# Block 1: the dilated attention's output projection in split products instead of f32 products

## The reference, cut to what matters

```python
ret = retention(rq, rk, rv, rg)
att = dilated_attention(aq, ak, av, rel_bias)
merged = jax.nn.sigmoid(ga) * (ret @ w_ret_o[l]) + jax.nn.sigmoid(gb) * (att @ w_att_o[l])
x = x + gt_a[:, None, :] * (merged @ w_o[l])
```

## Time and profile before

| | |
|---|---|
| median of 3 runs | 3548.91 us (3545.66 to 3554.22) |
| profiled execution, its own time | 3551.16 us |
| its span | 3549.2 us |
| mean granted PE clock over the span | 0.977 of full speed |
| PE busy | 3373.7 us, 95% of the span |
| DVE, ACT, POOL busy | 2045.4, 1772.0, 1048.0 us |

### The profile page before, as it was taken

The page is one execution under the profiler, slowest core; times in us unless marked ns, Lnnn a source line. Parts: engine busy times, 40 slices in busy tenths (PEclk is TensorE's granted clock), DMA queues, the critical chain, the costliest instruction groups (busy, mean ns, idle before and its releaser), DMA issues. The chain is left out here.

```text
span 3549.2 us, 54751 instructions
## 1 busy us (share of the span) xinstructions
PE 3373.7 (95%) x20660; PEld 2727.9 (77%) x20660; DVE 2045.4 (58%) x2356; ACT 1772.0 (50%) x2340; POOL 1048.0 (30%) x432
## 2 busy tenths in 40 slices
PE   7999999989999999999999898999999987799997
PEld 5888777768888888888888683778887866678876
DVE  3320121279999999999999725511153155446665
ACT  3222333258887878887888634432233342233333
POOL 2334222313222232323232140144443300034443
PEclk9999999989999999999999999999999988999999
DMA  8223443359999999999999637123322310022221
GB/s 288 85 72 101 125 125 125 112 207 383 375 381 374 385 368 386 367 386 371 381 378 377 249 111 280 66 83 97 99 89 72 101 37 4 7 72 95 96 95 42
DMA packets 247186, 696.26 MB, mean 196 GB/s; under 512 B 19806, under 2 KB 151634, under 8 KB 188420
## 3 DMA queue, kind: packets, MB, share of 16 engines
q1 hardware_dynamic: 237140, 658.52, 49.9%
q0 software_dynamic: 9792, 35.66, 3.8%
q10 hardware_dynamic: 112, 0.03, 0.0%
HBM read 668.90 MB, written 29.71 MB: 197 GB/s over the span
## 5 line engine op out<-in xcount | busy, mean ns | idle before, releaser
L340 POOL TENSOR_TENSOR split_w<-ring,split_w 128x1024 fp32r<-128x1024 f32 (+1 forms) x294 | 702.1, 2389 | 1581.6 <-ACT split_w L335 1505.3
L2272 DVE TENSOR_TENSOR moe_low<-ring,moe_high 128x2048 fp32r<-128x2048 f32 x408 | 929.4, 2285 | 56.6 <-ACT moe_high L2262 51.5
L2262 ACT ACTIVATE moe_high<-ring 128x1024 fp32r<-128x1024 f32 x810 | 833.6, 1063 | 123.4 <-PE psum L2513 121.9
L335 ACT ACTIVATE split_w<-ring 128x1024 fp32r<-128x1024 f32 (+1 forms) x294 | 304.4, 1036 | 978.4 <-PE psum L540 596.7
L2509 PE MATMUL psum<-moe_high,moe_xe 128*128 128x512 f32 x2176 | 585.2, 391 | 0.0
L2509 PEld LDWEIGHTS psum<-moe_high,moe_xe 128*128 128x128 f32 x2176 | 409.5, 188 | 82.2
L2421 POOL DMA_INDIRECT moe_y_rows<-moe_ye,moe_target x33 | 193.5, 5863 | 658.4 <-DVE moe_ye L2328 658.4
L540 PE MATMUL psum<-pair,split_w 128*128 128x512 f32 x1488 | 337.9, 389 | 0.0
L2513 PE MATMUL psum<-moe_low,moe_xe 128*128 128x512 f32 x1088 | 336.5, 390 | 0.1
L540 PEld LDWEIGHTS psum<-pair,split_w 128*128 128x128 f32 x1488 | 279.2, 188 | 58.8 <-issue 0.9
L540 PE MATMUL psum<-b_pair,split_w 128*128 128x512 f32 x1344 | 309.4, 391 | 0.0
(11 more groups left out here) (643 smaller groups left out, 4286.0 us busy)
## 6 DMA issues: line engine op xcount, KB each, us to landing
ring<-in_w_experts SPq DMA_DIRECT2D x408, 1024.0 KB, 8.7
ring<-in_w_mod SPq DMA_DIRECT2D x48, 1024.0 KB, 6.1
ring<-in_w_in SPq DMA_DIRECT2D x39, 1024.0 KB, 5.3
ring<-in_w_up SPq DMA_DIRECT2D x33, 1024.0 KB, 5.1
ring<-in_w_in SPq DMA_DIRECT2D x44, 512.0 KB, 5.2
ring<-in_w_down SPq DMA_DIRECT2D x20, 1024.0 KB, 5.1
ring<-in_w_gate SPq DMA_DIRECT2D x11, 1024.0 KB, 5.3
ring<-in_w_out SPq DMA_DIRECT2D x8, 1024.0 KB, 5.2
```

The costliest lines, as they stand in the source:

```text
L335: self.nc.scalar.activation(high, raw, ACT.Copy).then_inc(self.K.rounded, 1)
L340: self.nc.gpsimd.tensor_tensor(low, raw, high.bitcast(F32), ALU.subtract).then_inc(self.K.split, 1)
L2262: self.nc.scalar.activation(self.B["high"][:, j % HALVES, :], self.raw(j), ACT.Copy).then_inc(self.high, 1)
L2272: self.nc.vector.tensor_tensor(flat(self.low_of(j, 2)), self.K.ring[:, self.ring_slot(j // 2), :], high, ALU.subtract).then_inc(self.low, 2)
```

## The change

`att_o` joins `SPLIT`. Its weights (two chunks, four halves) are split as those of the other stages are; the first half is then split at the end of `gate_b`, and in `attention_out` ACT and POOL have the other three halves to split before they come to those of `w_o`. The rows of `attT` are split in `gate_b`: a new class `AttentionSplit` puts one Copy on ACT and one subtraction on DVE (128x512 each) into the steps (1, 0), (1, 1), (2, 0) and (2, 1). They go to a new tensor `b1_att_pair` (16 KB in each partition, beside `gb`). The projection's 32 f32 matmuls become 96 split ones, 24 to a half. PE waits for the last low part of `attT`, and for each half of the weights.

```diff
-SPLIT = ("ret", "gate_a", "ret_o", "att", "gate_b", "w_o", ...
+SPLIT = ("ret", "gate_a", "ret_o", "att", "gate_b", "att_o", "w_o", ...
...
+class AttentionSplit:
+    def __init__(self, K, attT, high, whole):
+        self.K, self.nc, self.attT, self.whole = K, K.nc, attT, whole
+        self.parts = (high[:, 0, :, :], high[:, 1, :, :])
+        self.high_at, self.low_at = {}, {}
+
+    def act_step(self, sc, j, i):
+        if j in (1, 2):
+            k = 2 * (j - 1) + i
+            if k == 0:
+                self.whole(sc)
+            self.K.act_link(self.nc.scalar.activation(self.parts[0][:, k, :], self.attT[:, k, :], ACT.Copy))
+            self.high_at[k] = self.K.act_order_n
+
+    def dve_step(self, ve, j, i):
+        if j in (1, 2):
+            k = 2 * (j - 1) + i
+            ve.wait_ge(self.K.act_order, self.high_at[k])
+            self.K.dve_link(self.nc.vector.tensor_tensor(self.parts[1][:, k, :], self.attT[:, k, :],
+                                                         self.parts[0][:, k, :].bitcast(F32), ALU.subtract))
+            self.low_at[k] = self.K.dve_order_n
...
-    linear_split(K, stage, "T", pair, 1, vacated=vacated,
+    linear_split(K, stage, "T", pair, 1, vacated=vacated, loads=loads, asked=True,
...
-def attention_out(K, attT, merge, source, vacated):
+def attention_out(K, x, merge, source, vacated):
...
-    ahead, evac0 = SplitAhead(K, last), K.dve_evac_n
+    W, evac0 = SplitWeights(K, "att_o"), K.dve_evac_n
...
         def _(sc):
-            ahead.high_ahead(sc)
+            for n, pieces in W.halves.items():
+                for _, _, place in pieces:
+                    W.act_high(sc, n, place)
+            W.high_ahead(sc)
             source.weights_high(sc)
             sc.wait_ge(K.dve_evac, evac0 + 1)
             for i in range(source.done):
...
         def _(po):
-            ahead.low_ahead(po)
+            W.pool(po)
             source.weights_low(po)
...
         def _(pe):
+            pe.wait_ge(K.dve_order, x.low_at[AH - 1])
             for j in range(2):
-                K.wait_chunk(pe, first + j)
                 vacated(pe, j)
-                w = K.slot(first + j)
-                for i in range(4):
-                    for k in range(AH):
-                        ins = nc.tensor.matmul(K.ps[:, 4 * j + i, :], w[:, k, i * P:(i + 1) * P], attT[:, k, :],
-                                               start=(k == 0), stop=(k == AH - 1))
-                ins.then_inc(K.chunk_used, 1)
+                for r0, nr, place in W.halves[first + j]:
+                    w = W.ready(pe, first + j, place)
+                    for i in range(4):
+                        for k in range(nr):
+                            for a, b in ((0, 0), (1, 0), (0, 1)):
+                                ins = nc.tensor.matmul(K.ps[:, 4 * j + i, :], w[:, a, k, i * P:(i + 1) * P],
+                                                       x.parts[b][:, r0 + k, :], start=(r0 + k + a + b == 0),
+                                                       stop=(r0 + k == AH - 1 and b == 1))
+                    W.used(ins, place)
             pe.wait_ge(K.dve_evac, evac0 + 1)
             source.products(pe)
```

More of the change, by code:

```diff
@@ L41 @@
 RWKV_C = 32
-SPLIT = ("ret", "gate_a", "ret_o", "att", "gate_b", "w_o", "b2_qkv", "b2_rest", "b2_out", "b2_up", "b2_down",
+SPLIT = ("ret", "gate_a", "ret_o", "att", "gate_b", "att_o", "w_o", "b2_qkv", "b2_rest", "b2_out", "b2_up", "b2_down",
          "b3_qk", "b3_v", "b3_rw", "b3_out", "b3_up", "b3_down")
@@ L1628, in retention, with sigmoid_gate @@
     return bias, vacated
-def sigmoid_gate(K, stage, pair, dst, vacated=None, room=None):
+def sigmoid_gate(K, stage, pair, dst, vacated=None, room=None, loads=None):
     def act(j, banks):
@@ L1954, in emptied @@
             pe.wait_ge(copied, 4 * AH)
-    return emptied
+    return emptied, lambda eng: eng.wait_ge(copied, 4 * AH)
+class AttentionSplit:
[17 more added lines that the diff above has]
+            self.low_at[k] = self.K.dve_order_n
 class RouteTables:
@@ L2813, in block1 @@
                                        lambda i: at_head + ATT_CHUNKS * (i // 2) + 5 + 2 * (i % 2), (7, 2), (0, 6))
-                        emptied = dilated(K, pair, attT, T0, T12, M, tables,
+                        emptied, whole_attT = dilated(K, pair, attT, T0, T12, M, tables,
                                           lambda pe, j: pe.wait_ge(K.dve_evac, dve0 + j + 1))
-                    with nc.sbuf_tensor("b1_gate_b", [P, KD, S], F32) as gb:
+                    with nc.sbuf_tensor("b1_gate_b", [P, KD, S], F32) as gb, \
+                            nc.sbuf_tensor("b1_att_pair", [P, 2, AH, S], F32R) as att_pair:
+                        parts = AttentionSplit(K, attT[:, :, :], att_pair[:, :, :, :], whole_attT)
                         act1, dve1 = K.act_evac_n, K.dve_evac_n
-                        sigmoid_gate(K, "gate_b", pair, gb, emptied, M.mods_ready)
+                        sigmoid_gate(K, "gate_b", pair, gb, emptied, M.mods_ready, parts)
                         def merge(j, banks):
@@ L2826, in block1 @@
                         source = SourceAhead(K, "w_o", merged, pair, 2)
-                        attention_out(K, attT, merge, source, lambda pe, j: pe.wait_ge(K.act_evac, act1 + 2 * j + 2))
+                        attention_out(K, parts, merge, source, lambda pe, j: pe.wait_ge(K.act_evac, act1 + 2 * j + 2))
             K.mods3 = K.later_ctx.enter_context(nc.sbuf_tensor("b3_mods", [P, 4, KD], F32, side="right"))
```

## The result

| | before | after |
|---|---|---|
| median | 3547.51 us (3542.89 to 3554.22, 19 runs) | 3554.69 us (3551.03 to 3558.66, 19 runs) |
| profiled execution, span | 3551.16, 3549.2 us | 3557.4, 3555.6 us |
| mean granted PE clock in the profiled execution | 0.977 | 0.975 |

The ratio is 1.0023, 95% interval [1.0017, 1.0029]: the changed kernel is **slower by 7 to 8 us** (the medians lie 7.18 apart; 0.0023 x 3548 is 8.2). The median lies 0.3 us inside the predicted range, which is luck: the range was made wide for other rivals and for scatter, not for this cause.

The account below looks back on a forecast made before the run. The prediction took PE's own work to bound the kernel. Matmuls −5.72, stall +5.0 and clock +1.72 summed to +1.0 us, a median of 3549.9 us, range 3545.0 to 3555.0.

Parts of the forecast that it names:

- The matmuls: Attention output projection on PE: four groups of 24 split matmuls take 21.76 us instead of 27.48, 5.72 us earlier.
- The rows of attT in the gate: Four ACT Copies and four DVE subtractions fit into idle time in the gate; cost 0, otherwise 2.5 us.
- The weights: Splitting the projection's weight halves on ACT and POOL: each is ready before PE asks; cost 0.
- Where PE then waits: Ahead of L457, PE idles 5.0 us for `w_o`'s place 1 and `merged`'s piece 0, with POOL holding DVE.
- The clock: In L457 behind the idle gap, PE falls to half rate and loses 1.72 us; bounds 0 and twice that.
- The sum: Whole program: −5.72 + 5.0 + 1.72 = +1.0 us, median 3549.9 us.
- 1: Ahead of L457, the stall comes without the clock's fall: −0.7 us, 3548.2; chance 0.15.
- 2: At the projection's end, PE doesn't wait and the whole gain arrives: −5.7 us, 3543.2; chance 0.06.
- 3: In the projection, the first merge holds POOL, making half 3 late: +2.8 us, 3551.7; chance 0.05.
- 4: In the dense output projection, the clock stays down: +9.1 us, 3558.0; chance 0.04.

Follow-up runs that it names:

- r3: Changed kernel with ACT splitting `merged` ahead of the weights that wait for the projection's last matmul; 0.9998 of the kernel before.
- r4: Changed kernel with 20 unread matmuls of 128x512 filling PE's gap ahead of L457; 1.0016 of the kernel before.
- s3: Changed kernel with 96 small unread matmuls in PE's gap ahead of L457, 128 more than the kernel before; 1.0003 of the kernel before.
- r2: Changed kernel run again unchanged, for a second trace; 1.0023 of the kernel before.
- s1: Kernel before the change with 32 small unread 32x32 matmuls ahead of L457; 1.0021 of the kernel before.
- t1: Changed kernel with ACT splitting `merged` first, plus 96 small matmuls where PE waits in block 1's routing; 0.9980 of the kernel before, median 3541.31 us.
- s4: Changed kernel with ACT splitting `merged` first, plus 96 small unread matmuls ahead of L457; 0.9998 of the kernel before.
- s2: Kernel before the change with 128 small unread matmuls ahead of L457; 1.0013 of the kernel before.

## Why the prediction was wrong, point by point

- **The matmuls**: right. −5.72 predicted; without the stall the stretch gives −5.75 (r3).
- **The rows of attT in the gate**: right, cost 0. DVE's subtractions took 0.69 to 2.48 us and were through near 640, as said.
- **The weights**: right. PE waited for no half inside the projection.
- **Where PE then waits**: right, instruction by instruction, an idle 4.81 us for 5.0; that POOL holds DVE was the better of the two bounds.
- **The clock**: right in kind, 1.48 for 1.72. r4 shows that the gap brought it on: with large matmuls in it L457 takes 5.72. With small ones in it the clock fell all the same (s3: 7.30).
- **The sum**: this is the step that failed. Its +1.0 us is the stretch's, and the stretch took +0.71 and +1.44. The step carried it over to the program as if nothing outside could change; the 32 matmuls more were priced by duration alone, and what they move behind them was put at nothing without a reason. It costs 5 to 7 us (the rests of r2, r3, r4 and s1), by the traces 5.5 of them in block 3, over 2000 us later. The prediction named "a difference that arises outside 613 to 735 us" as what would prove it wrong, and that is what happened; but it had given it no price and no chance, though rows of "issue" stand in the timeline of before. And the 0.2% that it took for what a measurement can tell was coarse: the interval of the result is 2 us to either side.
- **Rivals.** 1: wrong, the clock fell. 2: wrong for this kernel; with ACT's order changed the whole gain does arrive in the stretch, and in the program with t1. 3: POOL was not held, no L340 of the projection took over 2.40 us. The two did meet, but POOL began first (670.06 against 671.18), and it was the merge's addition that took 3.42 us instead of 2.29; nobody waited for it. 4: right in sign, wrong in its place: the dense projection came back to 1.00 inside L457, and the time at half rate came in block 3's bursts. That its +9.1 is near the measured 7 to 8 is chance.

## What to carry to other kernels

A change in the number of instructions on an engine moves everything behind it in that engine's stream. Where later stages run long bursts of very small instructions, price that too, and test it by itself: put as many cheap instructions into the old kernel (s1), and then as many as bring the later stages back to their old place (s3). In a loop only the first pass had such breaks here; whether a long burst gains from being written as one was not tried. And before a stall is filled with work, look whether the order on the engine that ends it can be changed: r3's one moved line shortened the stretch by 6.5 us (+0.71 to −5.75) at no price.

## What the hardware showed that I had not expected

- In bursts of matmuls some 15 ns apart (233 in 3.44 us) PE stood still for 1 to 2 us about every 128 or 256 matmuls, at places fixed in its program; moving these by 32 was worth 0.2% of the program, moving them by 128 nothing. In the later passes of a loop, with no packet on the instruction queue, it ran 256 in a row.
- Long rows of dense small matmuls did not keep the clock up: behind 96 of them without an idle gap L457 took 7.33 us (s4), and behind 128 the mean granted clock was 0.66 (s2), while PE was busy throughout. Behind 32 L457 took 5.73 (s1).
- POOL holds DVE for short operations too: a subtraction of 128x512 took 2.48 us beside a POOL operation and 0.69 alone (L1978, above).
